# Delta net: decay matrices made from spread rows, and the second step's system moved to the start of the first

## The chip, the cores and the metric

The kernel runs on one core of a Trainium2 chip. A core has TensorE (PE in the profile), VectorE (DVE), ScalarE (ACT), GpSimd (POOL) and SyncE (SP), which take their instructions in order, each from its own list, and wait for each other through semaphores. DMAs are issued from SP, ACT or POOL. The metric is the device time of one execution in microseconds (us), and less is better. Three runs of the kernel before took 1323.89, 1324.57 and 1327.45 us.

## The reference, cut to what matters

The program is a two-layer diffusion backbone over 256 latent and 256 context tokens of width 1024. Layer 0 mixes with a gated linear recurrence (RG-LRU) and with a gated DeltaNet in both directions. The part that the change touches is the DeltaNet's decay:

```python
def delta_chunked(q, k, v, beta, g, s0):
    gcum = jnp.cumsum(to_chunks(g[..., None])[..., 0], axis=-1)
    decay = jnp.exp(jnp.where(causal, gcum[..., :, None] - gcum[..., None, :], -jnp.inf))
    k_beta = kc * bc[..., None]
    m = jnp.where(strict, jnp.einsum('nbhid,nbhjd->nbhij', k_beta, kc) * decay, 0.0)
    sol = lax.linalg.triangular_solve(eye + m, rhs, left_side=True, lower=True, unit_diagonal=True)
    attn = jnp.einsum('nbhid,nbhjd->nbhij', qc, kc) * decay
    ...
    def step(S, xs):
        v_new = u_i - jnp.einsum('bhck,bhkv->bhcv', w_i, S)
        o = jnp.einsum('bhck,bhkv->bhcv', q_i, S) + jnp.einsum('bhij,bhjv->bhiv', attn_i, v_new)
        S = S * jnp.exp(gl)[..., None, None] + jnp.einsum('bhck,bhcv->bhkv', k_i, v_new)
```

`decay` is needed for every pair of tokens of a chunk, head and direction: it is the exponential of a difference of two cumulated log gates.

## The kernel before

Weights are streamed by SP in units of 128x1024 (`raw`), split by ACT into a high part `w_hi` (`split_hi`) and by DVE into a low part `w_lo` (`split_lo`), and PE multiplies three products of each (line 2770). A body of a projection is four units. Body 8 and body 9 of the joint list (`body_beside`; `LRU_TILES` is 8) are the two bodies of the projection `z`, and they end the input projection. Beside them run the squared sums of q and k (`l2_sums`, `l2_rstd`, `l2_load`, `l2_scaled`: ACT makes rows `l_rows`, writes them to DRAM and loads them back spread over all partitions as `l_four` and `l_fourth`; DVE multiplies q and k by them), and the DeltaNet's first system.

Then follows a loop of 8 steps over `q`, written out by hand on all engines. A step holds two chunks of 128 tokens and two heads in both directions. For each step there are:

- `decay(q)` on PE (line 3060): four products of 512 columns with masked log gates, `d_gu` and `d_gl`, which POOL makes in `log_gates` (line 838, four operations of 128x512). They leave log decay in a PSUM bank. `decay(q)` on ACT (line 1418) takes the exponential into `d_dt`.
- `k_k(q)` on PE (line 3048): k times k, which waits for that exponential, since it overwrites the same bank.
- `decayed_betas(q)` on POOL (`d_b`, line 845), `system(q)` on DVE (`d_n`, line 2311), `neighbours(q)` on DVE, PE and ACT (`near`), and `spread(q)` on POOL and DVE: a small elimination of 14 dependent operations on POOL, then `d_t` (line 617). This is the inverse within blocks of 8 tokens.
- four levels (8, 16, 32, 64) that double the blocks. At each level: `first_product` (PE, line 3169), `masked` (DVE, `d_pc`), `second_product` (PE, line 3178), `reduced` (DVE, into `d_t`), `gathered` (ACT, `d_tc`), `flip` (PE, line 3196), `flipped` (ACT, `d_tt`). The two chunks take turns.
- values, scores, states and outputs of step `q - 1`, between them.

Step `q` prepares the decay, system, neighbours and solve of `q + 1` while its own levels run. `mod_filler` puts modulation products (line 2696) into the step where `FILLERS` says. `row_loads` loads rows of exp(cumulated gates) from the DRAM tensor `eg_rows` into `d_qd`, spread over the partitions; the rows were written once by `beside`, in body 8.

The order of instructions on each engine is the order of the code, and a wait holds back everything behind it on that engine.

## Time and profile before

| | us |
|---|---|
| three runs | 1323.89, 1324.57, 1327.45 |
| the profiled execution | 1325.24 |
| its span in the profile | 1323.4 |
| PE busy | 1292.8 (98%) |
| DVE busy | 857.9 (65%) |
| ACT busy | 673.0 (51%) |
| POOL busy | 283.1 (21%) |

The span is the time between the first and last instruction that the profiler records; 1.84 us of the execution lie around it. Body 8 of the projection starts near 284 us, body 9 near 311 us, and the loop of 8 steps reaches from 336.6 to about 536 us. The TensorE clock is granted in full, at the level of 2.4 GHz, through all of this. A busy share says how full an engine is, and not what ends last; for that one looks at what each engine waited for, stretch by stretch.

### The profile page before, as it was taken

What the parts mean: (1) busy time and instruction counts of PE and PEld (TensorE: products, weight loads), DVE (VectorE), ACT (ScalarE), POOL (GpSimd) and SP (SyncE); (2) the same over time, 40 slices, a digit from 0 to 9 for tenths busy, and PEclk for the clock granted to TensorE, in tenths of its full rate; (3) what the DMA queues carried; (4) which work ended last, traced back from release to release, by engine and by line L of the source; (5) the groups of instructions that cost most, each with busy time, mean ns of one, the idle gap of its engine ahead of it and who ended that gap; (6) DMA issues with size and microseconds to landing.
All of it is one profiled execution on the core that took longest, in us unless ns stands there. A gap on an engine that the chain in (4) does not pass through costs nothing.

```text
span 1323.4 us, 27167 instructions
## 1 busy us (share of the span) xinstructions
PE 1292.8 (98%) x10915; PEld 1219.2 (92%) x10915; DVE 857.9 (65%) x1271; ACT 673.0 (51%) x1087; POOL 283.1 (21%) x360
## 2 busy tenths in 40 slices
PE   6999999999899999999999999999999999999998
PEld 3899899999798898999999999999999988999998
DVE  3764798996666675532777555666737666866663
ACT  4458888867545544313533211332236665664553
POOL 3000132422777886421000000000220001100002
PEclk8999999999999999999999999999999999999999
DMA  9632233225423112124466565555324221557662
GB/s 324 196 102 81 80 84 93 81 81 197 155 81 112 65 49 87 59 97 138 157 191 191 190 192 191 186 195 177 114 94 138 87 65 38 181 179 216 190 200 81
DMA packets 141308, 179.11 MB, mean 135 GB/s; under 512 B 11296, under 2 KB 122208, under 8 KB 140944
## 3 DMA queue, kind: packets, MB, share of 16 engines
q1 hardware_dynamic: 137312, 168.94, 40.6%
q10 hardware_dynamic: 3280, 8.46, 1.8%
q8 instruction: 78, 1.28, 0.4%
q0 software_dynamic: 608, 0.19, 0.1%
q14 instruction: 30, 0.25, 0.1%
HBM read 176.44 MB, written 1.11 MB: 134 GB/s over the span
## 4 chain that ended last, share of the span: by engine, by line
PE 77%; DVE 11%; ACT 5%; POOL 3%; issue 3%; DMA 1%; SPq 0%; DVEq 0%; ACTq 0%; POOLq 0%
PE bank L2770 55%; PE bank L2778 4%; DVE w_lo L1807 3%; DVE qkv L1893 2%; PE bank L3169 2%; PE bank L3178 2%; ACT w_hi L963 1%; PE bank L2696 1%; POOL qkv L821 1%; PE bank L3441 1%; PE bank L3464 1%; DMA first_w<-in_w_mod 1%; PE bank L3048 1%; PE bank L3107 1%; PE bank L3123 1%
## 5 line engine op out<-in xcount | busy, mean ns | idle before, releaser
L1807 DVE TENSOR_TENSOR w_lo<-raw,w_hi 128x1024 fp32r<-128x1024 f32 x212 | 265.5, 1253 | 297.6 <-ACT w_hi L963 297.4
L963 ACT ACTIVATE w_hi<-raw 128x1024 fp32r<-128x1024 f32 x212 | 223.5, 1056 | 378.2 <-PE bank L2770 376.4
L2770 PE MATMUL bank<-h_hi,w_hi 128*128 128x256 f32 x1472 | 298.4, 281 | 5.9 <-DVE w_lo L1807 3.4
L2770 PE MATMUL bank<-h_hi,w_lo 128*128 128x256 f32 x1472 | 293.6, 278 | 0.0
L2770 PE MATMUL bank<-h_lo,w_hi 128*128 128x256 f32 x1472 | 288.4, 278 | 0.0
L2770 PEld LDWEIGHTS bank<-h_hi,w_hi 128*128 128x128 f32 x1472 | 225.4, 188 | 14.7 <-issue 9.5
L2770 PEld LDWEIGHTS bank<-h_hi,w_lo 128*128 128x128 f32 x1472 | 225.3, 188 | 0.0
L2770 PEld LDWEIGHTS bank<-h_lo,w_hi 128*128 128x128 f32 x1472 | 222.4, 188 | 0.6 <-DVE h_lo L2107 0.4
L2770 PE MATMUL bank<-hid_hi,w_hi 128*128 128x256 f32 x768 | 171.9, 278 | 0.0
L2770 PE MATMUL bank<-hid_lo,w_hi 128*128 128x256 f32 x768 | 170.8, 277 | 0.0
L2770 PE MATMUL bank<-hid_hi,w_lo 128*128 128x256 f32 x768 | 170.7, 277 | 0.0
L789 POOL TENSOR_TENSOR n_sq<-xT 128x512 f32<-128x512 f32 (+1 forms) x18 | 17.1, 953 | 569.2 <-DVE xT L1922 568.5
L2770 PEld LDWEIGHTS bank<-hid_hi,w_hi 128*128 128x128 f32 x768 | 125.4, 188 | 1.6 <-issue 1.6
L2770 PEld LDWEIGHTS bank<-hid_lo,w_hi 128*128 128x128 f32 x768 | 125.5, 188 | 0.0
L2770 PEld LDWEIGHTS bank<-hid_hi,w_lo 128*128 128x128 f32 x768 | 125.3, 188 | 0.0
L1950 DVE SCALAR_TENSOR_TENSOR late_sum<-late_w,cs,late_sum 128x1024 f32<-128x1024 f32 x70 | 87.8, 1279 | 0.0
L2770 PE MATMUL bank<-mix_hi,w_hi 128*128 128x256 f32 x256 | 50.7, 280 | 0.0
L1893 DVE SCALAR_TENSOR_TENSOR qkv<-bank,vec,qkv 128x510 f32<-128x510 f32 (+1 forms) x72 | 48.3, 738 | 3.4 <-ACT qkv L1029 3.4
L2770 PE MATMUL bank<-mix_hi,w_lo 128*128 128x256 f32 x256 | 50.0, 277 | 0.0
L1061 ACT ACTIVATE hid_hi<-relu 128x512 f32 (+2 forms) x64 | 31.1, 517 | 36.4 <-DVE relu L1863 36.4
L821 POOL TENSOR_TENSOR qkv<-qkv,sigm 128x512 f32<-128x512 f32 x18 | 35.4, 2000 | 65.6 <-ACT sigm L1055 65.6
L2778 PE MATMUL bank<-rooted_hi,w_hi 128*128 128x256 f32 x160 | 44.5, 278 | 0.2
(381 smaller groups left out, 2401.7 us busy)
## 6 DMA issues: line engine op xcount, KB each, us to landing
raw<-in_mlp_w SPq DMA_DIRECT2D x128, 512.0 KB, 3.7
late_w<-in_w_mod SPq DMA_DIRECT2D x56, 512.0 KB, 4.4
raw<-in_even_w_in SPq DMA_DIRECT2D x48, 512.0 KB, 3.8
raw<-in_w_mod SPq DMA_DIRECT2D x24, 512.0 KB, 4.5
first_w<-in_w_mod SPq DMA_DIRECT2D x16, 512.0 KB, 11.1
raw<-in_even_w_out SPq DMA_DIRECT2D x16, 512.0 KB, 3.7
raw<-in_attn_w_qkv SPq DMA_DIRECT2D x16, 512.0 KB, 3.6
d_qd<-eg_rows ACTq DMA_DIRECT2D x16, 256.0 KB, 4.2
```

Source lines behind the costliest of these rows:

```text
L789: glink(pool.tensor_tensor(sq_[:, min(k, 1), 0:n], x_, x_, ALU.mult))
L821: pool.tensor_tensor(qkv[:, i], qkv[:, i], sigm[:, i % 2], ALU.mult).then_inc(s_silu, 1)
L963: act.activation(stored(w_hi, j, four), raw[:, j % RAW], ACT.Copy).then_inc(hi_ready, 1)
L1061: act.activation(bass_tok(hid_hi, it * 4 + (2 * pair + t), n0), relu[:, 2 * pair + t, 0:T - n0], ACT.Copy).then_inc(s_hid, 1)
L1807: dve.tensor_tensor(stored(w_lo, j, four), raw[:, j % RAW], stored(w_hi, j, four).bitcast(F32), ALU.subtract).then_inc(split_done, 1)
L1893: ins = dve.scalar_tensor_tensor(out=y[:, :, o0:o0 + w_], in0=x_[:, :, i0:i0 + w_], scalar=vec[:, bass.ds(tl + (VEC[cn] + j * nt_), 1)], i ...
L1950: ins = dve.scalar_tensor_tensor(out=acc[:, :], in0=late_w[:, x % RAW], scalar=cs[:, k, v:v + 1], in1=acc[:, :], op0=ALU.mult, op1=ALU.add)
L2696: mm = pe.matmul(bank[MODB][r0:r0 + 32, col:col + UNIT_C], cs[:, kk], w_[:, i], start=(kk == 0), stop=(kk == KT - 1), tile_position=(0, r0))
L2770: return pe.matmul(bank[2 * pair + t][:, c - n0:c - n0 + CTX], w_[:, k, t * P:(t + 1) * P], x_[:, c:c + CTX], start=(kk == 0 and first and ...
L2778: return pe.matmul(bank[2 * (j // s["upp"]) + t][:, 0:n], stored(w, j, True)[:, k, t * P:(t + 1) * P], h[:, kk, 0:n], start=(kk == 0 and f ...
L3169: mm = pe.matmul(out_, d_n[q % 2][:, 2 * c + i], slot_cols(q, 2 * c + i, LEVELS[l]), start=True, stop=True)
L3178: mm = pe.matmul(out_, d_tt[q % 2][:, 2 * c + i], d_pc[:, c, :, i], start=True, stop=True)
```

## The change

The log decay is no longer a matrix product. The cumulated log gates are turned into rows once, together with the exp rows, written to DRAM, and each step loads eight of them, spread over all partitions, into `d_lg` (`gate_rows`, ACT queue, 512 KB). ACT subtracts each token's own value from the four rows of one direction (`forward_gates`), DVE subtracts and takes the minimum with the other (`log_decay`), and ACT takes the exponential as before, now from SBUF. `g_tok` holds exp, value and negated value for each token (12 small activations instead of 4). PE's `decay`, POOL's `log_gates` and `sum_lines` are gone. `row_loads` is one DMA instead of two. In step 0, the second step's `k_k`, `system`, `neighbours` and `spread` are made at the beginning, `l2_scaled(3)` moves behind two levels, and two of the 24 modulation fillers move from step 0 to step 3.

```diff
-FILLERS = {0: {4: 2, 6: 2}, 1: {4: 2, 6: 2}, 2: {4: 2, 6: 2}, 7: {2: 2, 4: 2}}
+FILLERS = {0: {6: 2}, 1: {4: 2, 6: 2}, 2: {4: 2, 6: 2}, 3: {4: 2, 6: 2}, 7: {2: 2, 4: 2}}
...
@@ POOL
-            sum_lines()
...
-            log_gates(0, 1)
-            log_gates(0, 0)
             decayed_betas(0)
             spread(0)
-            log_gates(1, 1)
-            log_gates(1, 0)
...
                     decayed_betas(q + 1)
+                if q == 0:
+                    spread(1)
                 decayed_q(q)
...
-                if q + 2 < STEPS:
-                    log_gates(q + 2, 1)
-                    log_gates(q + 2, 0)
@@ ACT, body_beside and beside
                 if b == LRU_TILES:
+                    rows_out()
                     l2_load(0)
                 if ends:
                     l2_load(3)
+                    forward_gates(1)
                 evac(s, it, 0)
...
                     if b == LRU_TILES:
+                        decay(0)
                         l2_rstd(2)
...
+                if b == LRU_TILES and w == 2:
+                    gate_rows(0)
+                    gate_rows(1)
                 if b == LRU_TILES and w == 3:
                     act.preload_act_table_set("natural_log_exp_and_others")
                     l2_rstd(1)
-                    act.wait_ge(s_gps, 4)
-                    act.activation(eg_row[0:8 * STEPS, :], bank[X0][0:8 * STEPS, 0:P], ACT.Copy).then_inc(s_gate, 1)
-                    act.wait_ge(s_gate, 7)
-                    act.dma_start(eg_dram[:, :], eg_row[0:8 * STEPS, :]).then_inc(s_egw, 16)
+                    forward_gates(0)
                     betas(0)
-                    decay(0)
                     l2_load(1)
...
+            def rows_out():
+
+                act.wait_ge(s_gps, 4)
+                act.activation(eg_row[:, :], bank[X1][:, 0:P], ACT.Copy).then_inc(s_gate, 1)
+                act.wait_ge(s_gate, 7)
+                act.dma_start(eg_dram[:, :], eg_row[:, :]).then_inc(s_egw, 16)
+
+            def gate_rows(q):
+
+                if q == 0:
+                    act.wait_ge(s_egw, 16)
+                    act.wait_ge(l_out, 2)
+                elif q == 1:
+                    act.wait_ge(s_silu, BY_POOL)
+                else:
+                    act.wait_ge(a_dt, q - 1)
+                r_ = 8 * (STEPS + q)
+                act.dma_start(d_lg[q % 2][:, :, :, :].rearrange("p d i x -> p (d i x)"),
+                              eg_dram[r_:r_ + 8, :].rearrange("r x -> (r x)").partition_broadcast(P)).then_inc(s_rows_in[q % 2], 16)
+
+            def forward_gates(q):
+
+                act.wait_ge(s_rows_in[q % 2], rows_landed(q))
+                for i in range(4):
+                    r_ = 8 * q + 4 + i
+                    y_ = d_lg[q % 2][:, 1, i]
+                    ins = act.activation(y_, y_, ACT.Identity, bias=g_tok[:, NEG_LG, r_:r_ + 1])
+                alink(ins)
+                shifted[q] = acount[0]
+
             def decay(q):
 
-                act.wait_ge(p_dc, q + 1)
+                act.wait_ge(v_lg, q + 1)
                 if q >= 2:
                     act.wait_ge(g_at, 2 * q - 2)
-                act.activation(flat(d_dt[q % 2][:, :, :]), bank[R0 if q else R2][:, :], ACT.Exp).then_inc(a_dt, 1)
+                act.activation(flat(d_dt[q % 2][:, :, :]), flat(d_lg[q % 2][:, 0]), ACT.Exp).then_inc(a_dt, 1)
...
@@ ACT, the loop
                 flipped(q, LAST, 0)
+                if q + 2 < STEPS:
+                    forward_gates(q + 2)
                 tokens(q, 0)
@@ DVE, body_beside
                 if b < LRU_TILES + 1:
+                    if b == LRU_TILES:
+                        log_decay(0)
                     split_lo(u + 5, 5)
...
+            def log_decay(q):
+
+                dve.wait_ge(link_a, shifted[q])
+                dve.wait_ge(s_rows_in[q % 2], rows_landed(q))
+                for i in range(4):
+                    r_ = 8 * q + i
+                    y_ = d_lg[q % 2][:, 0, i]
+                    ins = dve.scalar_tensor_tensor(out=y_, in0=y_, scalar=g_tok[:, LG, r_:r_ + 1], in1=d_lg[q % 2][:, 1, i],
+                                                   op0=ALU.subtract, op1=ALU.min)
+                ins.then_inc(v_lg, 1)
...
@@ PE
-            def decay(q):
-
-                pe.wait_ge(g_gu, 2 * q + 2)
-                if q >= 2:
+            def k_k(q):
+                if q == 0:
+                    pe.wait_ge(s_gate, 6)
+                elif q >= 2:
                     pe.wait_ge(a_tok, 2 * q - 2)
-                elif q == 0:
-                    pe.wait_ge(g_gate, 2)
-                for d in range(2):
-                    for g_ in (d_gu, d_gl):
-                        mm = pe.matmul(bank[R0 if q else R2][:, :], lines[:, d], flat(g_[:, d]),
-                                       start=(d == 0 and g_ is d_gu), stop=(d == 1 and g_ is d_gl))
-                mm.then_inc(p_dc, 1)
-
-            def k_k(q):
-                pe.wait_ge(a_dt, q + 1)
                 four(R0 if q else R2, lambda i: feat(8, q, i), lambda i: feat(8, q, i)).then_inc(p_kk, 1)
...
+                    if UNIT_K * n + k == 8:
+                        pe.wait_ge(s_gate, 6)
+                        pe.transpose(bank[X1][:, 0:P], g_tok[:, EG:LG + 1].rearrange("p k r -> p (k r)"), C("ident")).then_inc(s_gps, 1)
...
             first_product(0, 0, 0)
             flip(0, -1, 0)
+            k_k(1)
...
-                if prep:
-                    decay(q + 1)
```

On ACT, in body 8, the rows of the gates are written behind the second product row of unit 2, and `l2_load(0)`, the load of `l_four`, comes behind them. `DMA eg_rows` is the write to DRAM, `DMA l_four` the load. Before:

```order
L1386 ACTIVATE eg_tok<-bank 128x4x4 x4
L1388 ACTIVATE neg_eg<-bank 128x64
L1388 ACTIVATE e_rest<-bank 128x64
L963 ACTIVATE w_hi<-raw 128x1024
L1346 DMA l_four<-l_rstd 128x2048
L1033 ACT_TABLE_LOAD
L1033 ACTIVATE siluz<-bank 128x512 x2
```

And in the changed kernel, on the same engine at the same place, to the end of `forward_gates(0)`:

```order
L939 ACTIVATE w_hi<-raw 128x1024
L1395 ACTIVATE eg_row<-bank 128x128
L1397 DMA eg_rows<-eg_row 128x128
L1325 DMA l_four<-l_rstd 128x2048
L1009 ACT_TABLE_LOAD
L1009 ACTIVATE siluz<-bank 128x512 x2
L1137 ACTIVATE qkv<-qkv 128x512 x2
L1409 DMA d_lg_102<-eg_rows 128x1024
L1409 DMA d_lg_103<-eg_rows 128x1024
L939 ACTIVATE w_hi<-raw 128x1024
```

The copy `eg_row` waits for PE's transpose, and the load of `l_four` has moved behind it and behind the write.

On DVE, at the start of step 0 (`d_pc` is `masked`, `d_t` is `reduced`, `d_n` is `system`, `vec` and `d_b` behind it are `neighbours`). Before:

```order
L2260 SCALAR_TENSOR_TENSOR qkv<-qkv,l_sq 128x1024 x2
L2305 TENSOR_TENSOR d_pc<-bank,cst 128x256
L2386 TENSOR_TENSOR d_t_106<-d_t_106,bank 128x2x16x8
L2311 SCALAR_TENSOR_TENSOR d_n_111<-bank,d_b 128x512
L2386 TENSOR_TENSOR d_t_106<-d_t_106,bank 128x2x8x16
L2305 TENSOR_TENSOR d_pc<-bank,cst 128x256
L2318 TENSOR_TENSOR d_b<-d_n_111,cst 128x512
```

In the changed kernel:

```order
L2338 SCALAR_TENSOR_TENSOR d_n_109<-bank,d_b 128x512
L2345 TENSOR_TENSOR d_b<-d_n_109,cst 128x512
L2332 TENSOR_TENSOR d_pc<-bank,cst 128x256
L2347 TENSOR_REDUCE vec<-d_b 128x32
L2413 TENSOR_TENSOR d_t_104<-d_t_104,bank 128x2x16x8
L2349 TENSOR_TENSOR d_b<-vec 128x256
L2413 TENSOR_TENSOR d_t_104<-d_t_104,bank 128x2x8x16
```

`system(1)` and the first part of `neighbours(1)` now stand ahead of the `masked` operation of level 1, and `l2_scaled(3)` (`qkv<-qkv,l_sq`) has left this place.

## Rows read from the trace of the kernel before

**Rows 1.** The page's first part: busy time and share of the span.
```profile
PE 1292.8 (98%) x10915; PEld 1219.2 (92%) x10915; DVE 857.9 (65%) x1271; ACT 673.0 (51%) x1087; POOL 283.1 (21%) x360
```

**Rows 2.** Windows of one loop step: PE, PEld, DVE, ACT, POOL busy, clock, DMA.
```profile
389.00:414.00 25.00, 24.75 (x221) 22.20 (x221) 17.39 (x37) 13.23 (x32) 18.13 (x30) 1.00 0.32 107
```

**Rows 3.** PE's waits, 289 to 361.3 us: us in total, times, longest.
```profile
PE bank L3169 <- POOL d_t L617: 1.9, 1, 1.9
PE bank L3178 <- ACT d_tt L1447: 1.3, 2, 1.0
```

**Rows 4.** PE's waits, 361.3 to 560 us.
```profile
PE bank L3060 <- POOL d_gl L838: 0.8, 2, 0.4
PE bank L3048 <- ACT d_dt L1418: 0.4, 1, 0.4
```

**Rows 5.** PE in order of time: start, us, line, operation, idle before it.
```profile
311.06 0.40 PE L2770 MATMUL bank<-h_hi,w_hi 128*128 128x256 f32 x2
...
338.40 0.68 PE L3178 MATMUL bank<-d_pc,d_tt 128*128 128x128 f32 x4 [0.97 <-ACT d_tt L1447]
...
339.65 0.50 PE L3060 MATMUL bank<-d_gu,lines 128*128 128x512 f32 x1
...
340.68 0.61 PE L3169 MATMUL bank<-d_t,d_n 128*128 128x128 f32 x4
...
349.94 1.07 PE L2696 MATMUL bank<-raw,cs 128*32 128x256 f32 x16
...
356.92 0.68 PE L3169 MATMUL bank<-d_t,d_n 128*128 128x128 f32 x4 [1.89 <-POOL d_t L617]
```

**Rows 6.** ACT in order of time, bodies 8 and 9 and the loop's start.
```profile
297.96 0.35 ACTq L1346 DMA_DIRECT2D l_four<-l_rstd  x1
...
313.70 0.69 ACT L1332 ACTIVATE l_rows<-bank,cst 128x512 f32<-128x512 f32 x1 [1.32 <-PE bank L3212]
...
322.01 0.38 ACT L1428 ACTIVATE near<-bank 128x256 f32<-128x256 f32 x1 [0.63 <-PE bank L3079]
...
322.29 0.38 ACT L1429 ACTIVATE near<-bank 128x256 f32<-128x256 f32 x1
...
324.97 1.65 ACT L1410 ACTIVATE d_b<-cst,beta,sp_x 128x128 f32<-128x128 f32 x4 [0.58 <-ACT l_rows L1333]
...
328.89 1.09 ACT L1033 ACTIVATE siluz<-bank 128x512 f32<-128x512 f32 x2
...
334.65 0.73 ACT L1174 ACTIVATE d_tc<-d_t 128x256 f32<-128x256 f32 x2 [2.16 <-POOL d_t L617]
...
337.87 0.39 ACT L1447 ACTIVATE d_tt<-bank 128x256 f32<-128x256 f32 x1
```

**Rows 7.** DVE in order of time, bodies 8 and 9.
```profile
305.84 2.36 DVE L2260 SCALAR_TENSOR_TENSOR qkv<-qkv,l_four 128x1024 f32<-128x1024 f32 x2 [2.94 <-DMA l_four<-l_rstd]
308.12 1.22 DVE L1807 TENSOR_TENSOR w_lo<-raw,w_hi 128x1024 fp32r<-128x1024 f32 x1
...
330.19 0.69 DVE L2260 SCALAR_TENSOR_TENSOR qkv<-qkv,l_four 128x512 f32<-128x512 f32 x1 [1.36 <-ACT siluz L1033]
...
333.34 2.36 DVE L1807 TENSOR_TENSOR w_lo<-raw,w_hi 128x1024 fp32r<-128x1024 f32 x1
```

**Rows 8.** DMA issues, 285 to 345 us: KB each, median us to landing.
```profile
l_four<-l_rstd ACTq DMA_DIRECT2D x2, 768.0 KB, 4.0
...
l_four<-l_rstd ACTq DMA_DIRECT2D x1, 1024.0 KB, 7.8
...
eg_rows<-eg_row ACTq DMA_DIRECT2D x1, 32.0 KB, 1.8
```

**Rows 9.** DVE in order of time, the state of one step.
```profile
384.33 1.12 DVE L2375 SCALAR_TENSOR_TENSOR d_s<-d_s,d_last,bank 128x128 f32<-128x128 f32 x4 [2.24 <-PE bank L3159]
```

**Rows 10.** ACT in order of time, where steps 0 and 2 end.
```profile
358.96 0.60 ACT L1441 ACTIVATE v_tok<-bank 128x512 f32<-128x512 f32 x1 [0.29 <-PE bank L3093]
...
408.97 0.60 ACT L1441 ACTIVATE v_tok<-bank 128x512 f32<-128x512 f32 x1 [1.18 <-PE bank L3093]
```

More of the change, by code:

```diff
@@ L433, in build @@
         solved = [0] * 8
+        shifted = [0] * 8
         dcount = [0]
@@ L937, in _ @@
                     lru_half(1)
-                if prep:
+                if prep and q:
                     spread(q + 1)
@@ L1384, in beside @@
                             x_ = eg_[:, 2 * cp:2 * cp + 2, d, :] if d else eg_[:, 2 * cp:2 * cp + 2, d, :][:, ::-1, :]
-                            y_ = eg_tok[:, :].rearrange("p (g e c a) -> p g e c a", e=4, c=2, a=2)[:, :, 2 * cp + d]
-                            act.activation(y_, x_.rearrange("p c (g a) -> p g c a", a=2), ACT.Exp)
+                            for k_, f_, by_ in ((EG, ACT.Exp, 1.0), (LG, ACT.Copy, 1.0), (NEG_LG, ACT.Copy, -1.0)):
+                                y_ = g_tok[:, k_].rearrange("p (g e c a) -> p g e c a", e=4, c=2, a=2)[:, :, 2 * cp + d]
+                                act.activation(y_, x_.rearrange("p c (g a) -> p g c a", a=2), f_, scale=by_)
                     for buf, c_ in ((neg_eg, 0), (e_rest, 64)):
@@ L1512, in _ @@
                     flipped(q - 1, LAST, 1)
-                if prep:
+                if prep and q:
                     decay(q + 1)
+                if q + 2 < STEPS:
+                    gate_rows(q + 2)
                 if q >= 2:
@@ L1522, in _ @@
                 if q == 0:
+                    neighbours(1)
                     split_hi(SEG["out"]["unit"] + 1, 1)
@@ L1528, in _ @@
                 gathered(q, 1, 1)
-                if prep:
+                if prep and q:
                     neighbours(q + 1)
@@ L1547, in _ @@
                 flipped(q, LAST, 0)
+                if q + 2 < STEPS:
+                    forward_gates(q + 2)
                 tokens(q, 0)
@@ L2045, in body_beside @@
                     spread(0)
+                    log_decay(1)
                 beside(b, 2)
@@ L2410, in _ @@
                 if q == 0:
-                    l2_scaled(3)
+                    system(1)
+                    neighbours(1, 0)
                 if tail:
@@ L2414, in _ @@
                 masked(q, 1, 0)
+                if q == 0:
+                    neighbours(1, 1)
                 reduced(q, 0, 1)
-                if prep:
+                if q == 0:
+                    neighbours(1, 2)
+                if prep and q:
                     system(q + 1)
@@ L2421, in _ @@
                 masked(q, 1, 1)
-                if prep:
+                if prep and q:
                     neighbours(q + 1, 0)
                 scores(q)
-                if q == 0:
-                    neighbours(q + 1, 1)
                 masked(q, 2, 0)
                 reduced(q, 1, 1)
-                if prep:
-                    if q:
-                        neighbours(q + 1, 1)
+                if prep and q:
+                    neighbours(q + 1, 1)
                     neighbours(q + 1, 2)
@@ L2440, in _ @@
                 masked(q, 2, 1)
+                if q == 0:
+                    l2_scaled(3)
                 if tail:
@@ L2455, in _ @@
                 reduced(q, 3, 1)
+                if q + 2 < STEPS:
+                    log_decay(q + 2)
             s_ = SEG["out"]
@@ L3076, in neighbours @@
                 pe.wait_ge(v_near, q + 1)
-                if q:
+                if q > 1:
                     pe.wait_ge(v_sc, q)
-                pe.matmul(bank[R0 if q else R2][:, 0:4 * LOCAL * LOCAL], C("local"), flat(d_b[:, 0:2]), start=True, stop=True).then_inc(p_near, 1)
+                elif q:
+                    pe.wait_ge(a_near, 2)
+                pe.matmul(bank[R0 if q > 1 else R2][:, 0:4 * LOCAL * LOCAL], C("local"), flat(d_b[:, 0:2]), start=True, stop=True).then_inc(p_near, 1)
             def tokens(q, i):
@@ L3228, in behind @@
                         gate_sums()
-                    if g == 1:
-                        pe.wait_ge(s_gate, 6)
-                        pe.wait_ge(l2["rs"], 1)
-                        pe.transpose(bank[X0][0:8 * STEPS, 0:P], eg_tok[:, :], C("ident")).then_inc(s_gps, 1)
-                        decay(0)
                     if g == 2:
@@ L3285, in _ @@
                 mod_filler(mods_in(q, 1))
-                if prep:
+                if prep and q:
                     k_k(q + 1)
@@ L3292, in _ @@
                 flip(q, 0, 1)
+                if q == 0:
+                    neighbours(1)
                 k_q(q)
@@ L3306, in _ @@
                 second_product(q, 2, 0)
-                if prep:
+                if prep and q:
                     neighbours(q + 1)
```

52 lines of the change are left out of this document (17 added, 35 removed).

## The prediction

> **What bounds the kernel now.** I read the page's busy shares first: PE is busy for 98% of the span, so a gain must come off PE's list or out of PE's few waits [rows 1]. Then the windows of a loop step: PE works 24.75 of 25 us, while DVE has 17.4, POOL 18.1 and ACT 13.2, all at the full clock [rows 2]. Then PE's waits in two stretches. Up to the end of step 0 it waits 1.9 us once for POOL's `d_t` and 1.3 us for ACT's `d_tt` [rows 3]. In the later steps it waits little, and 1.2 us of that is for POOL's gates and for the exponential made from them [rows 4]. The last views are the timelines of PE, ACT and DVE where the projection ends and the loop starts, because there the change adds work to ACT's list; the reader is to look at which instruction releases which.
>
> **What the change takes off PE.** A `decay` is four products, from 339.65 to 340.68, so 1.0 us [rows 5]. There are eight: one in body 8, one in step 0 and six in steps 1 to 6 (each makes the decay of the next step). PE works there without a gap, so the six are worth 6 x 1.0 = 6.0 us if nothing else comes late. The waits of [rows 4] go with them: 1.2 us. POOL loses four operations a step and is no bound.
>
> **What it adds on ACT and DVE.** `forward_gates` is four activations of 128x128 with one operand per partition. The trace does not show it. From below: two plain ones of 128x256 start 0.28 us apart, so four take 1.1 us. From above: four of 128x128 with two such operands take 1.65 us. I take 1.3, between the two [rows 6]. `log_decay` is four operations like those of the state: 1.1 us [rows 9]. The exponential stays at its size. The spread rows are 512 KB a step on a DMA share of 0.32 and are issued a step ahead: nothing.
>
> The Trainium skill (ScalarE: Activation LUTs, section What ACT_TABLE_LOAD costs) says that an activation takes 280 ns plus 0.833 ns per element with one pointer operand, and that neighbours overlap by 93 ns. By that rule four take about 1.2 us, as an estimate; no row here shows this form, and each of the two sums below would be better by 0.1 to 0.2 us.
>
> **The entrance (bodies 8 and 9).** The load of `l_four` is issued at 297.96 and its data release DVE at 305.84, after 2.94 us of idleness [rows 6, 7]. The change puts the copy of the gate rows ahead of it, which needs PE's transpose behind the first row of unit 2. By the pace of PE, 1.4 us a row, it ends near 298.9; with the transpose, the copy (0.3) and the issue of the write (0.5) the load goes out at about 300.3, so 2.3 us later. How late it lands is open: it took 7.8 us from issue to landing, a later one of 768 KB took 4.0 [rows 8]. So the landing is between 305 and 308; I take 307.3, because part of the 7.8 lay behind a weight load that is done by then. DVE is then 1.5 us late: its `w_lo` for the first unit of body 9 ends at 310.8 instead of 309.3. PE used it at 311.06 [rows 5, 7] and would now want it at 310.1, its decay product being gone. So the decay of body 8 buys 0.2 us, not 1.0, and the squared sums behind it come some 0.6 us later than before.
>
> ACT has little slack from there on. `forward_gates(0)` waits for rows that are issued at about 302.5, once the write has landed (1.8 us for half of it) [rows 8]; bounds 4.0 and 7.8 us give 306.5 to 310.3, and with the `l_four` ahead of them in the queue I take 309. `decay(0)` now waits for DVE's `log_decay(0)`, which stands behind two squares: 314.4, ahead of the third `l_rows`. The third `l_rows`, at 313.70 before [rows 6], starts at about 314.95: +1.25. Behind it are `w_hi`, `near`, the load of `l_fourth` and `betas(1)`; the load waits for `l2_scaled(1)`, which DVE does 1.7 us later, so about +1.4 at `betas(1)`. Then `forward_gates(1)` stands ahead of `siluz`, at 328.89 before: +1.3, so +2.6. That evacuation releases DVE's `l2_scaled(2)` (330.19), this POOL's `d_t`, this ACT's `d_tc` (334.65) and this, behind a table load and another evacuation, `d_tt` (337.87), for which PE waited 0.97 us at 338.40 [rows 5 to 7]. Nothing in this chain has slack beyond 0.2 us. So the first second product of the loop starts at 340.8 instead of 338.4. `k_k(1)` (0.9 us) fills part of the hole, and what is left of it is idle time.
>
> The trace has a `w_lo` of 1.22 us that took 2.36 beside POOL's `d_t` [rows 7]. The Trainium skill (GPSIMD Engine Reference, section Specifications) says that GpSimd shares its SBUF interfaces with VectorE and contends with instructions that have two SBUF inputs. `log_decay` has two, so `log_decay(1)` beside `d_t` could take 2.1 us instead of 1.1; it stands behind `spread(0)`, has the time of the table load and evacuation beside it, and by this rule the loop would start up to 0.5 us later still.
>
> **Step 0.** Before, 18.5 us passed from that second product to the first product of step 1 (356.92), 1.9 of them the wait for `d_t` [rows 3, 5]. The change takes from this stretch a decay (1.0), `k_k(1)` (0.9), a filler pair (1.0) [rows 5] and the wait. But the levels of step 0 are a chain through DVE and ACT, and DVE's list now has `system(1)` and part of `neighbours(1)` ahead of the level's `masked`: `system(1)` needs `decay(1)` on ACT (behind a table load of 1.3) and POOL's `d_b` (1.3), so `masked` comes 5.0 us after the second product, where the next product went at 4.5 before. ACT's `w_hi` slides ahead of a `gathered` (+1.0), and `l2_scaled(3)`, 2.35 us, now stands between two levels. Walking the four levels with the old durations, I get 17.9 us. So step 1's first product comes at 358.7, +1.8 against before.
>
> **Ends of steps.** `forward_gates(q + 2)` stands ahead of `v_tok`. At the end of step 0 ACT was idle 0.29 us before it and PE waited for it already: +0.9. In steps without a state product there ACT idled 1.18 us [rows 10]: +0.2, three times, 0.6. In the others a state product hides it. The filler pair that left step 0 is paid in step 3: +1.0.
>
> **The sum.** +1.8 (entrance and step 0) + 0.9 + 0.6 + 1.0 - 6.0 - 1.2 = -2.9 us against the profiled execution of 1325.24, so 1322.3. That execution was 0.7 above the median of the runs, 1324.57; against the median it is 1321.7.
>
> **Rivals.** *Full gain.* The entrance is hidden: `l_four` lands as early as before and ACT takes the added work into its waits of 1.3 and 2.2 us [rows 6]. Then the loop starts at 338.4 with `k_k(1)` done, step 0 gains the wait for `d_t` and about a decay, and the sum is 8.0 + 1.9 less 0.9 and 0.6 for the ends of steps = -8.4 us: 1316.2. For it: ACT is only half busy, and each delay that I chain hangs on a landing that I estimate. Against it: the row of 0.97 us shows ACT releasing PE at just this place.
>
> *The levels bound the loop.* PE looks full because its list is ordered to cover the level chain; without the decay it waits for `d_t` and `d_tt` instead, and only half of the 6.0 comes back. Sum: +0.1, so 1324.7. For it: PE does wait for DVE's `d_t` here and there. Against it: DVE waits much more for PE than PE for DVE.
>
> *Slower: the rows land late on ACT's list.* `forward_gates(0)` waits with `betas(0)`, the next load and `w_hi` behind it. If each of the two loads takes the 7.8 us of `l_four`, one behind the other, the rows of step 0 land near 314 instead of 309. Then `w_hi` and `w_lo` for body 9's second unit are late for PE, every later link by 5 us more, and the sum is +2.1 plus 2 to 3 for `w_lo`: +4.6, 1329.2. It decides against the change as soon as the loop's first second product starts later than about 343.7, which is 340.8 plus the 2.9.
>
> That the change does not do what it says can be left out: the products are gone from the order.
>
> **How the numbers follow.** A measurement of this kernel can tell 0.3%, 4.0 us, from no change. The forecast, near -2.9, has 0.44; full gain 0.34; the levels 0.12; slower 0.10. The predicted time is that of the forecast, 1321.7. The unknown costs are 1.5 us of landing, 0.3 to 0.5 per `forward_gates`, and 2 us in my walk of step 0, so its own range is 1318.5 to 1325. The range of eight in ten takes in the full gain and the levels: 1315.5 to 1327. Faster by over 0.3% (below 1320.6): the full gain and a fifth of the forecast, 0.42. Slower: the last rival, and not always past the bound, 0.10. The same: 0.48.
>
> **What would show it.** Right: no line of decay products; the first `l2_scaled` about 1.5 us later; PE's first second product of the loop at 340 to 341.5 with an idle stretch ahead of it for `d_tt`; `siluz` of body 9 about 2.6 us later; steps 1 to 6 about 1 us shorter each. Wrong: the loop starting at 338.4 or before, or steps that are no shorter while PE waits for `d_t`, `d_tt` or `v_tok`.

## The result, and the profile after

The changed kernel takes 1333.53 us (median of 9 runs, 1330.60 to 1339.01) against 1324.57 (9 runs, 1322.64 to 1328.86): ratio 1.006, 95% interval 1.0045 to 1.0074. It is slower by 9.0 us where 2.9 less were forecast, and lies above the range given.

The first part of the page after the change, beside [rows 1]:

```profile
PE 1292.0 (97%) x10883; PEld 1219.1 (91%) x10883; DVE 875.5 (66%) x1303; ACT 681.6 (51%) x1127; POOL 247.6 (19%) x323
```

PE has 32 instructions fewer and yet only 0.8 us less busy time: part of its work ran at a lower clock. POOL lost 35.5 us. DVE has 17.6 us more, although the 32 operations of `log_decay` at 0.28 us would make 9.

To see where the time went I put the two traces side by side at points that both have: the starts of ACT's high split `w_hi` (the 18th, 24th, 45th, 49th and 51st of the list, here w17, w23, w44, w48, w50), the first `d_tt` of the loop on ACT, and DVE's scores (`d_dt`) of steps 1 and 7. Each number of this table is the difference of two starts. What lies ahead of w17 and behind w50 has the same instructions in the same order. The whole times scatter there: in the kept traces the stretch ahead of w17 takes 131.8 to 135.3 us, and the one behind w50 takes 781.0 to 783.4 us in ten of them and 785.8 to 786.7 in five (e6, e7, e8, e10 and e12, where PE does 214 products in 25 us instead of 223 at a granted clock of 1.00), so the whole time of a single run settles nothing below 5 us.

| stretch | before | after | e2 | e9 | e10 | e11 |
|---|---|---|---|---|---|---|
| w17 to w23 (projection) | 40.56 | 42.94 | 42.76 | 42.76 | 40.55 | 40.58 |
| w23 to w44 | 128.11 | 128.48 | 128.56 | 128.58 | 128.52 | 128.49 |
| w44 to w48 (bodies 8, 9) | 27.90 | 29.11 | 28.76 | 28.81 | 28.95 | 27.52 |
| w48 to first `d_tt` | 6.44 | 6.73 | 6.74 | 6.74 | 6.74 | 6.82 |
| `d_tt` to scores 1 (step 0) | 30.92 | 34.24 | 31.40 | 34.93 | 34.87 | 32.52 |
| scores 1 to scores 7 | 146.48 | 148.32 | 148.22 | 143.56 | 143.26 | 143.37 |
| scores 7 to w50 | 26.37 | 26.29 | 26.37 | 26.29 | 26.37 | 26.37 |
| sum | 406.78 | 416.11 | 412.81 | 411.67 | 409.26 | 405.67 |

So 9.3 us are lost in four places: 2.4 at 160 to 170 us, far ahead of the DeltaNet; 1.9 from w23 up to the first `d_tt`; 3.3 in step 0; and 1.8 in steps 1 to 6, which were to become 6 us shorter.

**160 to 170 us.** DVE and POOL of the changed kernel in order of time (start, duration, engine, line, operation, idle before it and its releaser; so in all timelines below):

```profile
164.54 3.46 POOL L822 TENSOR_TENSOR qkv<-qkv,sigm 128x512 f32<-128x512 f32 x2
```

```profile
164.55 2.35 DVE L2248 TENSOR_TENSOR_SCAN l_b<-l_a,l_b 128x512 f32<-128x512 f32 x1
166.83 2.25 DVE L1820 TENSOR_TENSOR w_lo<-raw,w_hi 128x1024 fp32r<-128x1024 f32 x1
...
177.01 1.23 DVE L2237 TENSOR_TENSOR l_b<-l_i,xc 128x1024 f32<-128x1024 f32 x1
```

`gate_parts` lost its two casts, so POOL comes to its products of q, k and v two operations earlier, and these now lie beside DVE's scan and `w_lo`, which take 2.35 and 2.25 us. Experiment e1 shows the same two at 1.22 and 1.20. The single records look as if the two engines took turns: POOL's first product ends at 165.82, the scan at 166.91, POOL's second product at 167.99 and `w_lo` at 169.07.

**Entrance and step 0.** PE of the changed kernel, beside [rows 5]:

```profile
339.69 0.68 PE L3194 MATMUL bank<-d_t,d_n 128*128 128x128 f32 x4 [0.77 <-POOL d_t L615]
...
343.12 0.68 PE L3203 MATMUL bank<-d_pc,d_tt 128*128 128x128 f32 x4 [1.63 <-ACT d_tt L1456]
...
345.64 0.41 PE L3221 MATMUL bank<-cst,d_tc 128*128 128x128 f32 x2 [0.61 <-ACT d_tc L1150]
...
348.37 1.22 PE L3203 MATMUL bank<-d_pc,d_tt 128*128 128x128 f32 x4 [1.88 <-DVE d_pc L2332]
349.81 1.22 PE L3194 MATMUL bank<-d_t,d_n 128*128 128x128 f32 x4 [0.21 <-DVE d_t L2413]
...
352.10 1.91 PE L3081 MATMUL bank<-qkv 128*128 128x128 f32 x8
...
360.72 0.71 PE L3203 MATMUL bank<-d_pc,d_tt 128*128 128x128 f32 x4 [1.57 <-DVE d_pc L2332]
```

Windows of the same place (busy PE, PEld, DVE, ACT, POOL; clock; DMA share; GB/s):

```profile
340.00:350.00 10.00, 5.66 (x39) 4.82 (x38) 6.24 (x12) 6.03 (x11) 1.57 (x3) 0.91 0.49 157
350.00:360.00 10.00, 8.46 (x46) 7.69 (x46) 6.21 (x11) 5.90 (x15) 5.84 (x14) 0.74 0.13 35
```

And in the kernel before:

```profile
340.00:350.00 10.00, 8.69 (x66) 7.43 (x68) 9.36 (x17) 4.71 (x11) 5.50 (x7) 1.00 0.15 52
350.00:360.00 10.00, 7.52 (x77) 5.70 (x77) 3.44 (x9) 5.69 (x16) 8.72 (x19) 1.00 0.88 296
```

PE waits 0.77, 1.63, 0.61 and 1.88 us in 10 us. Behind that the granted clock is 0.74 over 10 us, so it is at its level of 1.2 GHz for part of them: a group of four that takes 0.61 to 0.71 us takes 1.22. What this costs can be bounded from traces with the same step 0: over the 20 us around it (from 344 us here) the granted clock is 0.83 in the changed kernel and in e1, where the stretch from `d_tt` to scores 1 takes 34.24 and 34.20 us, and 0.91 in e7 and e4, where it takes 33.64 and 34.00. So half of the lost clock is worth 0.2 to 0.6 us.

ACT of the changed kernel, beside [rows 6, 10]:

```profile
333.83 1.09 ACT L1009 ACTIVATE siluz<-bank 128x512 f32<-128x512 f32 x2
...
342.58 0.39 ACT L1456 ACTIVATE d_tt<-bank 128x256 f32<-128x256 f32 x1
...
365.15 0.33 ACTq L1507 DMA_DIRECT2D d_qd<-eg_rows  x1
365.52 0.38 ACT L1456 ACTIVATE d_tt<-bank 128x256 f32<-128x256 f32 x1 [4.08 <-POOL d_qd L867]
...
366.90 1.26 ACT L1418 ACTIVATE d_lg<-d_lg,g_tok 128x128 f32<-128x128 f32 x4
368.19 0.60 ACT L1450 ACTIVATE v_tok<-bank 128x512 f32<-128x512 f32 x1
```

The load of `d_qd` for step 1 waits for POOL's `decayed_q(0)`, which the change put behind the whole of `spread(1)` (POOL's `d_qd` starts at 362.62 and takes 2.50 us). It holds back ACT's list for 4.08 us.

**A later step.** DVE and POOL of the changed kernel where step 1 ends, beside [rows 9]:

```profile
391.05 2.89 DVE L2316 SCALAR_TENSOR_TENSOR d_lg<-d_lg,g_tok 128x128 f32<-128x128 f32 x4 [0.92 <-ACT d_lg L1418]
393.86 1.11 DVE L2402 SCALAR_TENSOR_TENSOR d_s<-d_s,d_last,bank 128x128 f32<-128x128 f32 x4
```

```profile
390.70 2.56 POOL L855 TENSOR_TENSOR d_at<-d_dt,cst 128x512 f32<-128x512 f32 x2 [1.61 <-PE bank L3173]
```

PE's waits in the steps, 367.4 to 565 us (us in total, times, longest), beside [rows 4]:

```profile
PE bank L3132 <- DVE d_s L2402: 3.1, 4, 0.9
PE bank L3104 <- DVE d_b L2349: 2.0, 4, 0.7
PE bank L3118 <- ACT v_tok L1450: 2.0, 4, 1.1
PE bank L3194 <- DVE d_t L2413: 1.9, 5, 0.6
```

`log_decay` is four operations of the size of the state's, which take 1.11 us. Where it starts beside POOL's `d_at` it takes 2.82 to 2.89, five times over; the state behind it comes late, and PE waits for `d_s`. By single records two of the four are held: they end at 392.13 and 393.41, each 0.14 us behind one of POOL's two `d_at` (391.99 and 393.27), and the other two take 0.34 each. Between scores 1 and 7 PE is busy for 140.70 of 148.32 us; before the change it was busy for 143.51 of 146.48. So its idle time grew from 3.0 to 7.6 us where products were taken away.

The Trainium skill (GPSIMD Engine Reference, section Specifications) says that GpSimd shares its SBUF interfaces with VectorE and contends with instructions that have two SBUF inputs. The traces agree at both places, and they add what it costs: 1.1 us each for scan and `w_lo`, and 1.7 to 1.8 for the four of `log_decay`. The ends above show this as a wait for the end of the neighbour's operation, not as a slower pace.

### The profile page after: what moved, and what is told of

Read it like the earlier page. It is cut to its first block, busy times and chain, and to the rows that moved or that the text cites. A ratio compares the mean times of both kernels' runs of the same rounds, so it can differ in the third digit from the quotient of the medians.

```text
span 1334.2 us, 27140 instructions
## 1 busy us (share of the span) xinstructions
PE 1292.0 (97%) x10883; PEld 1219.1 (91%) x10883; DVE 875.5 (66%) x1303; ACT 681.6 (51%) x1127; POOL 247.6 (19%) x323
## 3 DMA queue, kind: packets, MB, share of 16 engines
q8 instruction: 78, 1.28, 0.4%
## 4 chain that ended last, share of the span: by engine, by line
PE 75%; DVE 11%; ACT 6%; issue 3%; POOL 2%; DMA 2%; SPq 0%; ACTq 0%; DVEq 0%; POOLq 0%
PE bank L2803 54%; PE bank L2811 5%; DVE w_lo L1820 2%; DVE qkv L1906 2%; PE bank L3194 2%; PE bank L3203 1%; PE bank L2729 1%; POOL qkv L822 1%; PE bank L3465 1%; ACT w_hi L939 1%; DMA first_w<-in_w_mod 1%; PE bank L3488 1%; DVE d_lg L2316 1%; PE bank L3132 1%; PE bank L3148 1%
## 5 line engine op out<-in xcount | busy, mean ns | idle before, releaser
L3203 PE MATMUL bank<-d_pc,d_tt 128*128 128x128 f32 x256 | 40.1, 279 | 7.1 <-ACT d_tt L1456 3.5
```

The lines of the kernel that those rows point to most:

```text
L3203: mm = pe.matmul(out_, d_tt[q % 2][:, 2 * c + i], d_pc[:, c, :, i], start=True, stop=True)
```

## The experiments

Two theories. Mine after the comparison: *the level chain and the neighbours' delays*. The decay products lay in waits of the chain of levels, so taking them away gives almost nothing, and what was added stands in the chain itself (`log_decay`, `forward_gates`, ACT's held list, POOL's earlier start). The rival: *PE's list*. The products were worth their time, and something else in step or entrance (the clock, the late `l_four`) ate it. The verdicts are read from the stretches of the table. Scores 1 to 7 took 148.22 to 148.36 us in the changed kernel and in four runs that leave this stretch alone or add to its idle time (e2, e4, e7, e8), but 149.25 in a fifth (e1); step 0 repeats within 0.6 us. Six experiments ran once only, with these whole times: e5 1320.40, e6 1332.36, e7 1340.08, e8 1337.14, e12 1333.36 and e13 1327.93 us.

**e1, the two casts back.**

```diff
                 pool.wait_ge(s_gate, 5)
+                glink(pool.tensor_copy(g_hi[:, :, :], g_log[:, :, :]))
+                pool.tensor_tensor(g_lo[:, :, :], g_log[:, :, :], g_hi[:, :, :].bitcast(F32), ALU.subtract)
```

> The changed kernel with POOL's two casts g_hi and g_lo put back into gate_parts (nobody reads them), so that its gated products start about 2.3 us later again. Theory: the casts' absence let those products fall beside DVE's scan and w_lo of 160 to 170 us, which took 2.3 us each instead of 1.2; with the casts back w_hi of split 23 starts 2.2 us earlier again and the whole is 2.2 us shorter, 1331.3 us. Rival: the 2.2 us are swallowed by the waits where the loop of the DeltaNet starts (landings there don't move with it): 1333.5 us, with the start of split 23 earlier and the loop's start not.

DVE of e1:

```profile
161.69 1.22 DVE L2252 TENSOR_TENSOR_SCAN l_b<-l_a,l_b 128x512 f32<-128x512 f32 x1
162.83 1.20 DVE L1824 TENSOR_TENSOR w_lo<-raw,w_hi 128x1024 fp32r<-128x1024 f32 x1
```

w17 to w23 takes 40.56 us, as before the change: 2.4 us back. In all 1332.25 us, ratio 1.0063 (1.0042 to 1.0083): 1.3 less than the changed kernel, which these runs can't tell from nothing or from 2.2. The stretch up to w50 is 1.7 shorter; between the scores of steps 4 and 5 it takes 1.2 more, and 0.3 less in the step ahead of that. Two operations that no one reads make the kernel's front faster: shown. That all of it stays: not shown by this run, but see e9 and e10.

**e2, decayed_q(0) first.**

```diff
+                decayed_q(q)
                 if q == 0:
                     spread(1)
-                decayed_q(q)
```

> The changed kernel with POOL's decayed_q(0) ahead of spread(1), as before the change. Theory: ACT's d_qd load for step 1 waits for decayed_q(0), which stands behind the elimination of spread(1), and holds ACT for 4.1 us; without that, the end of step 0 is 3 to 4 us earlier: 1330 us. Rival: the lost time of step 0 is in its level chain and in the slower TensorE clock, and ACT's 4.1 us only stand in front of another wait (for v_tok): within 1 us of the changed kernel, 1332.5 to 1333.5 us.

ACT of e2, at the same load:

```profile
358.03 0.33 ACTq L1507 DMA_DIRECT2D d_qd<-eg_rows  x1
359.13 0.38 ACT L1456 ACTIVATE d_tt<-bank 128x256 f32<-128x256 f32 x1 [0.69 <-PE bank L3221]
```

1329.80 us, ratio 1.0042 (1.0025 to 1.0060), and step 0 is 2.84 us shorter (34.24 to 31.40). The theory holds; of the 3.3 us that step 0 lost, one line explains 2.8 (of these, 0.2 to 0.6 can be the clock's by the bound above: it is 0.91 and 0.92 in 340 to 360 us, where the change has 0.91 and 0.74).

**e3, step 0 in its old order on all engines.** `k_k(1)`, `system(1)`, `neighbours(1)`, `decay(1)` on ACT, `spread(1)`, `l2_scaled(3)` and the fillers at their old places, the decays as in the change. (Two places of the edit are shown.)

```diff
+                if prep:
+                    k_k(q + 1)
-FILLERS = {0: {6: 2}, 1: {4: 2, 6: 2}, 2: {4: 2, 6: 2}, 3: {4: 2, 6: 2}, 7: {2: 2, 4: 2}}
+FILLERS = {0: {4: 2, 6: 2}, 1: {4: 2, 6: 2}, 2: {4: 2, 6: 2}, 7: {2: 2, 4: 2}}
```

> The changed kernel with step 0 in the order of before on all engines (second step's k_k, system, neighbours, spread at their old places, l2_scaled(3) and the fillers too); the decays stay those of spread rows. Theory: of the 5 us that step 0 loses about 4 to 5 come back, and TensorE's granted clock stays at 1.0 through it: 1328.5 to 1329.5 us. Rival: the entrance (2.84 + 1.9 us late) and the idle time there lower the clock whatever the order of step 0: 1332 to 1334 us, with a granted clock below 0.9 in 350 to 360 us.

1331.41 us, ratio 1.0060 (1.0037 to 1.0083). Step 0 takes 32.87 us: 1.4 better than the change and 1.5 worse than e2. The clock falls here too, and earlier:

```profile
330.00:340.00 10.00, 6.69 (x56) 6.32 (x55) 6.71 (x10) 7.26 (x13) 1.83 (x1) 0.90 0.43 127
340.00:350.00 10.00, 8.78 (x56) 8.43 (x55) 8.33 (x12) 4.50 (x10) 6.54 (x7) 0.75 0.40 143
```

PE waits 2.53 us for `d_tt` up to 339.54, and the clock has fallen before that wait ends. So both were half right: only 2.1 us of the 4 to 5 came back, and the clock falls with the old order too, though in 350 to 360 us, where the rival had put it, it is 1.00. That the late entrance brings it down was argued and not tested. The new order of step 0 itself shows no loss: e3 has the filler pair of 1.0 us in step 0 and is 1.5 longer there, and takes 0.7 of it back from scores 3 to 4 (25.50 us instead of 26.16), where e2 has the pair.

**e4, four products more in steps 1 to 6.**

```diff
                 mod_filler(mods_in(q, 0))
+                if prep and q:
+                    pe.wait_ge(a_tok, 2 * q)
+                    four(R0, lambda i: feat(8, q + 1, i), lambda i: feat(8, q + 1, i))
```

> The changed kernel with four products more (k times k once more, 0.9 to 1.06 us, nobody reads this first result) in steps 1 to 6 at the place where the decay products stood. Theory (the levels bound the loop, PE's list has waits in place of the decays): the steps take the products into those waits, 1333.5 to 1335.0 us. Rival (PE's list bounds, the decays' time came off and something else was added): 6 x 1.0 = 6 us more, 1339.5 us.

Scores 1 to 7 take 148.25 us against 148.32, and from the first `d_tt` to scores 7, with all six groups in it, 182.25 against 182.56; in all 1332.84 us. Six times 0.9 us of products cost nothing: PE's idle time between scores 1 and 7 falls from 7.6 to 3.3 us instead. At this place in the list, PE does not bound the steps. It is not so at every place, as the filler pair of e3 shows: 0.7 us for 1.0.

**e5, the other side: three of four decay products left out of the kernel before.**

```diff
-                for d in range(2):
-                    for g_ in (d_gu, d_gl):
+                for d in range(1 if q >= 2 else 2):
+                    for g_ in ((d_gu,) if q >= 2 else (d_gu, d_gl)):
```

> The kernel before with one of the four decay products left out of every three of four: from step 1 on each decay makes one product of 512 columns instead of four (the decays of the third and later steps are then incomplete), 0.75 us less of PE's work a step in steps 1 to 6; nothing is added anywhere. Theory (the chain of levels bounds the steps even before the change): from the scores of step 1 to those of step 7 the loop takes 146.5 us as before, within 1 us. Rival (PE's list bounded the loop before, and what the change adds on DVE and ACT took its place): 6 x 0.75 = 4.5 us less, 142.0 us.

Scores 1 to 7 take 145.49 us against 146.48: 0.99 less. Five of the six shortened decays stand in this stretch (3.75 us); the sixth, ahead of scores 1, gave nothing (31.00 us from the first `d_tt` instead of 30.92). In all 0.9 of 4.5 us. It comes from one step: scores 2 to 3 take 24.06 us instead of 24.91, and the other five together are 0.14 shorter. That one is nearly the window of [rows 2], with PE busy for 24.75 of 25 us. So before the change the products were worth their time in that step and next to nothing in the others, though from scores 1 to 2 PE was as busy (24.06 of 24.30 us). This is one run; e1 has a step that is 1.2 us longer without a cause in it.

**e6, no forward_gates and log_decay from the third step on.** Their six calls are gone; the exponential waits for the load instead.

> The changed kernel without forward_gates and log_decay for the third and later steps (their decays are then exponentials of the bare rows, so the output is another). It takes 1.3 us off ACT's list and 1.1 to 2.9 us off DVE's at the end of steps 0 to 5. Theory (these two, placed at the turn of the steps, and log_decay taking 2.9 us beside POOL's d_at, cost what the products' absence gives): from the scores of step 1 to those of step 7 it takes 1 to 1.8 us a step less than the 148.3 of the changed kernel, 138 to 142 us. Rival (the levels alone set the pace): 147.5 to 148.3 us.

143.63 us, above the 138 to 142 expected and far below the rival's. That is 4.7 less than with them and 2.85 less than before the change: what the absence of the products, of POOL's gates and of the waits on both is worth if the replacement were free. The filler pair that came to step 3 lies in it with 0.7 (e3), so they are worth some 3.6 us, of 6.2 that were forecast for them in this stretch (five decays of 1.0 and 1.2 of waits).

**e9, the pair half a step earlier.**

```diff
@@ ACT
                 gathered(q, 2, 0)
                 if q + 2 < STEPS:
+                    forward_gates(q + 2)
                     betas(q + 2)
...
                 flipped(q, LAST, 0)
-                if q + 2 < STEPS:
-                    forward_gates(q + 2)
                 tokens(q, 0)
@@ DVE
                 if tail:
                     rest_of_v(q - 1, 1)
+                if q + 2 < STEPS:
+                    log_decay(q + 2)
                 masked(q, 3, 0)
...
                 reduced(q, 3, 1)
-                if q + 2 < STEPS:
-                    log_decay(q + 2)
```

> The changed kernel with forward_gates ahead of the betas and log_decay ahead of the masked of the last level, half a step earlier, where ACT waits 1.2 us and DVE 2.2 us, and where POOL has only its small solve instead of d_at. Theory: log_decay takes 1.1 to 1.5 us instead of 2.9, the state product behind it and PE's wait for d_s of 0.9 us go, and steps 1 to 6 are 0.7 to 1 us shorter each: 148.3 less 4 to 6 from the scores of step 1 to those of step 7, 1328 to 1329.5 us in all. Rival (the level chain has the same length wherever the pair stands): 147.5 to 148.3 us and 1332.5 to 1334 us.

143.56 us for scores 1 to 7: all of what e6 gains, with nothing left out. `log_decay` in e9:

```profile
406.19 1.38 DVE L2315 SCALAR_TENSOR_TENSOR d_lg<-d_lg,g_tok 128x128 f32<-128x128 f32 x4
```

The place was the cost, not the work. Step 0 takes 0.7 more: `log_decay(2)` stands behind `l2_scaled(3)` there and ahead of the last level, takes 2.31 us, and PE waits 3.85 us for the `d_pc` behind it. In all 1333.39 us (4 runs, 1329.02 to 1335.51), ratio 1.0071 (1.0043 to 1.0100): the expected 1328 to 1329.5 was missed by the median, while the profiled run of 1329.02 has the gain in its trace. The other three have no kept trace, so where their time went stays open; e10 and e11 have the same stretch and more runs.

**e12, forward_gates alone moved.** The first half of the edit of e9.

> The changed kernel with forward_gates alone moved to where e9 has it, log_decay still at the end of the step, beside POOL's d_at. Theory (log_decay beside d_at is what costs the steps; ACT's part is cheap): DVE starts log_decay some 0.9 us earlier without its wait for ACT, it still takes 2.3 to 2.9 us, and the steps from the scores of step 1 to those of step 7 take 146.5 to 148 us, so most of e9's gain (143.6) is missing. Rival (forward_gates ahead of v_tok on ACT is what costs): 143.5 to 145 us.

145.52 us: above the rival's range by 0.5 and below the theory's by 1.0. Moving `forward_gates` gives 2.8, and moving `log_decay` as well another 2.0. `log_decay` still takes 2.15 to 3.23 us there, but starts earlier. So the loss of 4.7 is ACT's four activations ahead of `v_tok` and `d_tt`, and DVE's slow four behind them, in this proportion if ACT's are moved first; the other order was not run.

**e7, l_four ahead of the gate rows.** `l2_load(0)` and `rows_out()` change places.

> The changed kernel with the load of l_four issued ahead of the write of the gate rows, as early as before the change. Theory (by the changed trace, the load's wait costs only 0.4 us up to the second unit of body 9, since landing took 5.1 us instead of 7.8): from split 23 to split 44 128.1 to 128.3 us instead of 128.5, and the loop starts 0 to 0.4 us earlier, 1333.2 us. Rival (the prediction's term: the late load of l_four carries through to the loop's start): 1.5 us or more earlier.

Wrong for both: w23 to w44 takes 129.73 us, 1.25 more, and w23 to the first `d_tt` 165.29 instead of 164.32. `l_four` lands 1.9 us earlier, but the rows of `d_lg` are issued later and hold ACT:

```profile
306.19 1.70 ACTq L1409 DMA_DIRECT2D d_lg<-eg_rows  x2
308.00 1.06 ACT L939 ACTIVATE w_hi<-raw 128x1024 fp32r<-128x1024 f32 x1 [1.64 <-issue]
```

The changed kernel issues them in 0.82 us at 304.79 and `w_hi` follows at 306.74. The order of the change is the better one here.

**e8, PE kept busy in step 0.** e2 with three groups of four products more (`four(R1, ...)`) at PE's waits.

> The kernel of e2_dq_first with three further groups of four products (nobody reads them, 0.9 to 1.06 us each at 2.4 GHz) in step 0, in front of the second products at which PE waits 1.6 and 1.9 us, and at the first k_q. Theory: PE's waits are filled, TensorE's granted clock stays at 1.0 in 340 to 360 us, and from the first d_tt of the loop to the scores of step 1 it takes 0.5 to 1.5 us less than the 31.4 of e2. Rival (the clock's fall lies beside waits and costs nothing, the added products cost their time): 31.4 to 33 us.

Step 0 takes 31.92 us against 31.40, and the clock is 0.95 and 0.88 in 340 to 350 and 350 to 360 us, where e2 has 0.91 and 0.92. The products did not keep the clock, and the stretch is 0.5 us longer, as the rival had it.

**e10 and e11, the repairs together.** e10 is e1, e2 and e9. e11 keeps `log_decay(2)` at the end of step 0 and moves `forward_gates(1)`:

```diff
                     l2_load(3)
-                    forward_gates(1)
                 evac(s, it, 0)
...
                 beside(b, 3)
                 if ends:
+                    forward_gates(1)
                     gathered(0, -1, 0)
```

> Three edits at once on the changed kernel: the two POOL casts back (e1), decayed_q(0) ahead of spread(1) (e2), forward_gates and log_decay half a step earlier (e9). Theory: the three act in different places and add up: -2.2, -2.9 to -3.3 and -3.7 to -4.7 (e9 lost 1.0 of its 4.7 in step 0, where log_decay stood behind l2_scaled(3)), so 8.8 to 10.2 us off 1333.5: 1323.3 to 1324.7 us. Rival (a gain at one of the places is taken back at the next wait): 1326 us or more.

> e10 with two more: log_decay(2) stays at the end of step 0, and forward_gates(1) moves from ahead of siluz to ACT's idle time of 2.7 us two instructions later in body 9. Theory: siluz and the first d_tt of the loop come 0.8 to 1.1 us earlier, and the last level of step 0 is not held by log_decay: 1 to 2 us below e10, 1321.5 to 1323.5 us, the only version at or below the kernel before (1324.6). Rival (the loop's start waits for POOL's d_t and table loads rather than for forward_gates): as e10 within 0.5 us.

The kernel before took 1327.64 us on that chip, so the ratios and the stretches decide. e10: 1328.88 us (12 runs), ratio 1.0019 (1.0000 to 1.0038), 2.5 us above the kernel before by the ratio and by the table and 1.2 by the medians, where the sum said 1.3 below to 0.1 above. The front (40.55) and the steps (143.26) have their gains, but step 0 takes 34.87: `log_decay(2)` ahead of the last level takes the place of the wait that e2 had removed, with 3.85 us of PE waiting for `d_pc` as in e9. The rival held.

e11: 1323.68 us against 1327.64 (12 and 23 runs), ratio 0.9978 (0.9961 to 0.9996). It is the only version ahead of the kernel before, by 1.1 us in the table. Against e10 it gains 3.6 us in the table, more than the 1 to 2 expected. ACT of e11 where body 9 ends:

```profile
329.18 1.09 ACT L1013 ACTIVATE siluz<-bank 128x512 f32<-128x512 f32 x2
...
332.15 1.28 ACT L1422 ACTIVATE d_lg<-d_lg,g_tok 128x128 f32<-128x128 f32 x4
335.01 0.73 ACT L1154 ACTIVATE d_tc<-d_t 128x256 f32<-128x256 f32 x2 [1.58 <-POOL d_t L617]
```

`forward_gates(1)` now lies in ACT's wait for POOL's `d_t`, and w44 to w48 is 1.4 us shorter than in e10. Step 0 is 2.35 shorter.

**e13, the four products of e4 in e11.**

> The version of e11 with the four extra products of e4 in steps 1 to 6 (k times k once more, nobody reads it). Theory (after the pair is moved the level chain has slack against PE's list, so PE bounds the steps again): from the scores of step 1 to those of step 7 it takes 3 to 6 us more than the 143.4 of e11, where in e4 it was nothing. Rival (the chain of levels bounds also here): under 1.5 us more.

144.86 us against 143.37: 1.5 us for the five groups of 0.9 in this stretch, at the rival's bound. The sixth stands ahead of scores 1, where the time from the first `d_tt` is 34.10 us instead of 32.52; a part of that can be the clock, as above. So here the products cost up to 3.1 of 5.4 us where they cost nothing in the change: with the pair moved, both the levels and PE's list count.

## Why the prediction was wrong, step by step

- **What the decay products are worth: the step that failed.** "PE works there without a gap, so the six are worth 6 x 1.0 = 6.0 us", and 1.2 for the waits of [rows 4]. Measured: 0.9 of 4.5 us for the products alone (e5), some 3.6 of 6.2 with POOL's gates and the waits (e6 and e3), and e4 puts six groups back for nothing. The window of [rows 2] was read as a bound for all the steps. It shows nearly the one step in which e5 gives the whole time back; in the others PE's list fills the waits of the level chain, and when a piece goes, the wait under it comes to light. There was a gap, too: PE was idle for 3.0 us between scores 1 and 7. The third rival said that half would come back, and got 0.12; that half is what e6 and e3 give. Against it I held that DVE waits more for PE than PE for DVE; in a chain through three engines each waits for the one before it, so that says nothing.
- **What `forward_gates` and `log_decay` cost: mis-sized by place.** The four activations took 1.26 to 1.28 us (1.3 forecast), right. (The rule of the Trainium skill that the prediction quotes, from ScalarE: Activation LUTs, section What ACT_TABLE_LOAD costs, gives 4 x 387 - 3 x 93 ns = 1.27 us as an estimate, not 1.2, and agrees with the traces.) But "+0.2, three times" for the place ahead of `v_tok` was too little, and `log_decay` behind `reduced` of the last level was priced at nothing. Together 4.7 us (e6, e9): 2.8 for the first, 2.0 for the second (e12, in that order). The shared interface was weighed for `log_decay(1)` beside `d_t` (2.20 us measured there, 2.1 by that rule), and not asked for at the turn of the steps, where POOL's `d_at` stands. Forecast for steps 1 to 6: -6.0 - 1.2 + 0.6 + 1.0 = -5.6; for scores 1 to 7, which hold five of the six decays, -4.6. Measured +1.8.
- **The casts.** They were not priced at all; "POOL loses four operations" was looked at as a bound only. Their absence costs 2.4 us 130 us ahead of the DeltaNet (e1).
- **The entrance.** `l_four` released DVE at 308.01, 2.2 later in the trace and 0.7 earlier once the 2.8 us that were there at w23 are taken off, against +1.5; it took 5.1 us to land instead of 7.8. So the landing term of 1.5 did not come true: the third `l_rows` starts at 316.14, 2.4 later in the trace and 0.4 earlier without those 2.8, against +1.25. The end of the chain did: `siluz` of body 9 was to be 2.6 later. It starts at 333.83 instead of 328.89, 4.9 later and 2.1 without the 2.8. The first second product was to be 2.4 later: it is 4.7 later, and 1.9 without those 2.8. `forward_gates(1)` ahead of `siluz` is carried through as forecast, since e11 takes 1.35 us back by moving it; what makes up the rest was not tested. That the sum of 1.9 lies near 2.4 is in part luck.
- **Step 0.** From that second product to step 1's first product 17.9 us were forecast instead of 18.5; the trace has 19.9 (343.12 to 363.02). Level 1's `masked` started 4.77 us after the second product (347.89; 5.0 forecast), and its product 5.25. What was missed: ACT's wait of 4.08 us for `decayed_q(0)` behind `spread(1)`, worth 2.8 (e2), and the low clock, 0.4 to 1.2 us by the bound above (an estimate). I had listed every instruction that moved, but not the semaphore that another engine's list waits on.
- **The slower rival.** It said 1329.2, with late rows on ACT's list, from a first second product later than 343.7. That came at 343.12, so its mechanism did not decide; e7 shows that those rows do hold ACT when they are later still. The sign was its, by other causes. Its chance of 0.10 was too small for a change that touches four engines' lists.

The ledger: 2.4 (casts) + 6.4 (scores 1 to 7, +1.8 instead of -4.6) + 3.5 (from w23 to scores 1, 5.2 instead of 1.8 + 0.9 - 1.0 for the sixth decay) = 12.3 us, against the distance of 12.2 between -2.9 forecast and +9.3 in the traces.

## What to carry to other kernels

A list that is 99% busy may be full because it was packed around a chain, and one full step does not speak for its neighbours; before you sell an instruction's time, find the wait it covers in each step, or put a copy of it in and see whether it costs anything. Price what replaces it by where it stands and by what the neighbour engine does in that moment, not only by its length. And when an operation leaves or moves on one engine, follow everything behind it: who meets it now, and whose wait sits on a semaphore that it raises.

## What the runs showed of the hardware

- DVE operations with two SBUF operands beside a POOL operation of the same kind: 128x512 scan 1.22 to 2.35 us, `w_lo` of 128x1024 1.20 to 2.25, four subtract-minimum operations of 128x128 1.14 to 2.89. The added time is a wait for the end of POOL's operation: ends at 391.99 and 393.27 (POOL) are followed by ends at 392.13 and 393.41 (DVE). It went both ways at one place and not at the other: POOL's two products at 164.54 took 3.46 us instead of 2.56 in e1, while its two `d_at` took 2.55 to 2.56 beside `log_decay` and, up to step 6, 2.49 to 2.51 in e9.
- An activation of 128x128 with one operand per partition takes 0.39 us alone; four take 1.26 to 1.28.
- Four waits of 0.6 to 1.9 us in 10 us were followed by a granted clock of 0.74 over 10 us (1.2 GHz for part of it). In e3 the clock fell during a wait of 2.53 us, with 0.90 and 0.75 in the two windows. Before the change a wait of 0.97 and one of 1.07 us, 9.6 us apart, left it at 1.00.
